# A 21,000-instruction fp32 block on one core: halves, quarters and casts moved between engines at the stage joints

## What is computed

```python
# first_block
h = x
h += chunked_band_attention(rmsnorm(h, norm_mix[0]))              # 16 heads
h += sq_relu_mlp(rmsnorm(h, norm_mlp[0]), w1[0], w2[0])            # relu(h@w1)**2 @ w2, width 4096
h += rglru_block(rmsnorm(h, norm_mix[1]))                          # conv, gates, scan, gelu branch, @ w_o
h += sq_relu_mlp(rmsnorm(h, norm_mlp[1]), w1[1], w2[1])
x = rmsnorm(h, norm_final)
# second_block
y = rwkv7_time_mix(rms_norm(x, norm_pre[0]), ...) ; h = x + rms_norm(y @ w_out, norm_post[0])
h += rms_norm(sigmoid(h @ ple_gate[0]) * (p[0] @ ple_w[0]), ple_norm[0])
k, v = shared_kv(h); y = diff_attention_mix(rms_norm(h, norm_pre[1]), k, v, ...)
h += rms_norm(y @ w_out, norm_post[1])
h += rms_norm(sigmoid(h @ ple_gate[1]) * (p[1] @ ple_w[1]), ple_norm[1])
```

## Time and profile before

| | |
|---|---|
| median of 3 executions | 1169.71 us (1169.52 to 1169.93) |
| the profiled execution | 1173.79 us, its span 1172.0 us |
| mean granted TensorE clock in it | 0.988 of full |
| PE busy | 1113.3 us (95%), 8956 instructions |
| DVE, ACT, POOL busy | 475.7 us (41%), 540.0 us (46%), 707.8 us (60%) |
| DMA | 169.44 MB, 145 GB/s in the mean |
| products of line 203 (fillers) | 500 of a 128 x 128 constant by the page, 59.4 us busy |

### The profile page before, as it was taken

The page is one execution under the profiler, slowest core; times in us unless marked ns, Lnnn a source line. Parts: engine busy times, 40 slices in busy tenths (PEclk is TensorE's granted clock), DMA queues, the critical chain, the costliest instruction groups (busy, mean ns, idle before and its releaser), DMA issues. The chain is left out here.

```text
span 1172.0 us, 20965 instructions
## 1 busy us (share of the span) xinstructions
PE 1113.3 (95%) x8956; PEld 925.5 (79%) x8956; DVE 475.7 (41%) x647; ACT 540.0 (46%) x851; POOL 707.8 (60%) x443
## 2 busy tenths in 40 slices
PE   9999999999999899999999999899998889999895
PEld 8788799998899789989984445899847677777864
DVE  1125274333246646521137175535641350233332
ACT  6437364444458755544421151212222564559452
POOL 5975459988947599998820035300034849667770
PEclk9999999999999999999999998999999989999998
DMA  8661455555546355555572443000036425433240
GB/s 319 225 233 55 144 159 184 189 188 189 189 129 212 110 162 183 191 186 193 183 233 72 127 158 110 21 4 4 4 127 236 150 95 183 140 100 120 81 159 36
DMA packets 45852, 169.44 MB, mean 145 GB/s; under 512 B 5088, under 2 KB 5344, under 8 KB 45440
## 3 DMA queue, kind: packets, MB, share of 16 engines
q1 hardware_dynamic: 43312, 159.06, 41.3%
q0 software_dynamic: 2448, 9.05, 2.4%
HBM read 167.03 MB, written 1.05 MB: 143 GB/s over the span
## 5 line engine op out<-in xcount | busy, mean ns | idle before, releaser
L709 POOL TENSOR_TENSOR ring_r<-ring,high_r 128x512 fp32r<-128x512 f32 (+1 forms) x368 | 636.6, 1763 | 238.9 <-ACT high_r L868 223.8
L868 ACT CAST high_r<-ring 128x1024 fp32r<-128x1024 f32 x248 | 256.2, 1049 | 215.6 <-DMA ring<-w 213.5
L435 PE MATMUL psum<-x_high,high_r 128*128 128x256 f32 x640 | 182.4, 285 | 2.2 <-DVE x_low L290 2.2
L435 PE MATMUL psum<-x_low,high_r 128*128 128x256 f32 x640 | 181.1, 283 | 0.0
L435 PE MATMUL psum<-x_high,ring_r 128*128 128x256 f32 x640 | 181.1, 283 | 0.0
L409 PE MATMUL psum<-high_r,x_high 128*128 128x512 f32 x320 | 127.3, 398 | 2.5 <-POOL ring_r L709 1.5
L612 DVE TENSOR_TENSOR arena<-arena 128x512 f32<-128x512 f32 x32 | 54.8, 1713 | 179.6 <-ACT arena L588 179.5
L435 PEld LDWEIGHTS psum<-x_high,high_r 128*128 128x128 f32 x640 | 122.7, 192 | 3.5 <-issue 1.8
L409 PE MATMUL psum<-high_r,x_low 128*128 128x512 f32 x320 | 124.8, 390 | 0.0
L409 PE MATMUL psum<-ring_r,x_high 128*128 128x512 f32 x320 | 124.6, 389 | 0.0
L435 PEld LDWEIGHTS psum<-x_low,high_r 128*128 128x128 f32 x640 | 122.7, 192 | 0.5
(11 more groups left out here) (317 smaller groups left out, 1717.2 us busy)
## 6 DMA issues: line engine op xcount, KB each, us to landing
ring<-w SPq DMA_DIRECT2D x292, 512.0 KB, 3.4
row<-rows POOLq DMA_DIRECT2D x14, 512.0 KB, 7.1
arena<-relt SPq DMA_DIRECT2D x2, 1536.0 KB, 10.6
h<-x SPq DMA_DIRECT2D x1, 1024.0 KB, 5.0
arena<-lora POOLq DMA_DIRECT2D x2, 512.0 KB, 6.8
out<-h SPq DMA_DIRECT2D x1, 1024.0 KB, 4.0
con<-consts SPq DMA_DIRECT2D x1, 529.0 KB, 4.5
arena<-pT POOLq DMA_DIRECT2D x2, 256.0 KB, 4.8
```

Source lines behind the costliest of these rows:

```text
L435: ins = nc.tensor.matmul(out, a, b, start=(k == 0 and q == 0), stop=(k == KT - 1 and q == 2))
L709: ins = nc.gpsimd.tensor_tensor(low(m)[:, part], raw(m)[:, part], read(high(m))[:, part], ALU.subtract)
L868: nc.scalar.copy(high(m), raw(m)).then_inc(high_made, 1)
```

## The change

1. **MLP ends.** The last four `w2` pieces are multiplied bank by bank: (tile 0, half 0), (0, 1), (1, 0), (1, 1), twelve products each, and each bank is announced by itself. The four pieces are released in the last of these. VectorE adds, ScalarE sums squares by half tile, VectorE finishes tile 0's statistics and scales it, and TensorE transposes tile 0 and then tile 1; fillers of 22 and 31 become 6 and 16. Behind the second MLP the two norms' roots are taken together, and transposes go to four banks instead of two.
2. **Recurrent block's end.** `a` squared and the casts of pieces `y6`, `y7` and the first of `W_RO` move from ScalarE to VectorE; ScalarE's tanh needs no settling wait. The first half's products with the gelu branch stand before the second half's scans; ScalarE's remaining casts lie between its gelus. GpSimd makes `W_RO`'s first low part without waiting for the scans. The filler of 34 and the wait before it are gone.
3. **Time mix.** The products of line 1939 come in three groups of 12, 12 and 8 instructions, each after a piece of `v`. `T_YA` is transposed, evacuated and used by halves, its first half ahead of the last gate piece; the filler of 8 is gone.
4. **Embedding.** The loop over the two rows of `p` is outside, that over the column halves inside, both column halves read from pieces 0 and 1; `piece_used` rises by 1 after the first row and by 3 after the second. Of pieces 2 and 3 eight columns are loaded.
5. **Rows.** GpSimd loads gain rows 11 to 13 later, in its list of the second attention.
6. **Second attention's end.** The first half of the heads is gated and transposed inside the loop, the SiLU of the last gates comes after the last heads' scaling, ScalarE's last two casts after the heads' root; GpSimd's `combine(7)` and `gate_rows(1)` move one piece forward; the filler of 30 becomes 5 and that of 16 is gone; the projection takes the halves as they come.
7. One filler of 7 in the chunk core becomes 8.

```diff
+UNUSED_PIECES = {4 * n + i for n in (W_PLE0, W_PLE1) for i in (2, 3)}
@@ mlp_act
-            split_until(min(w2_piece(m, 7, 3) + 1 + AHEAD, 4 * W_RKVG))
+            split_until(min(w2_piece(m, 7, 0) + RING, 4 * W_RKVG))
@@ mlp_pe
+            for t in range(NT):
+                for half in range(2):
+                    for f in range(4):
+                        piece_ready(pe, w2_piece(m, 7, f))
+                        pe.wait_ge(z_low, 16 * m + 14 + f // 2 + 1)
+                        ins = w2_product(m, 7, f, t, half)
+                        if (t, half) == (1, 1):
+                            ins.then_inc(piece_used, 1)
+                    if (t, half) != (1, 1):
+                        ins.then_inc(w2_part, 1)
@@ gpsimd
-            low_until(4 * W_RO)
+            low_until(4 * W_RO + 1)
...
-            for r in range(10, 14):
-                load_row(r)
+            load_row(10)
...
-                                   (33, combine, 6), (35, combine, 7), (36, gate_rows, 1)):
+                                   (33, combine, 6), (34, combine, 7), (35, gate_rows, 1)):
@@ scalar, recurrent block
-                settle(ins)
-                nc.scalar.activation(bb_[:, 4 * q:4 * q + 4, :], aa[:, 4 * q:4 * q + 4, :], ACT.Square).then_inc(g_ready, 1)
+                ins.then_inc(g_ready, 1)
...
+            made[0] = 4 * W_RO + 1
+            act.wait_ge(high_made, SPLITS[4 * W_RO + 1])
+            branch(0)
+            branch(1)
+            split_until(4 * W_RO + 3)
+            og_high_part(0)
+            og_high_part(1)
+            branch(2)
+            split_until(4 * W_RO + 5)
+            branch(3)
@@ vector, recurrent block
+                dve.wait_ge(a_ready, q + 1)
+                settle(nc.vector.tensor_tensor(bb_[:, u, :], aa[:, u, :], aa[:, u, :], ALU.mult))
...
+                for m in ((REC_AT["y6"], REC_AT["y7"]), (4 * W_RO,))[q]:
+                    cast_piece(m)
...
+                if q == 0:
+                    og_product(0)
+                    og_product(1)
@@ scalar, gates
-                split_until(4 * W_OUT_A + 4 * j + 4)
+                split_until(4 * W_OUT_A + 2 * j + 4)
+                evacuate_high(act, T_YA, (XH, None), blocks=(2 * j, 2 * j + 1))
@@ tensor
-            hold_clock(4, 22)
-            pe.wait_ge(xn_ready, 1)
-            pe_transposes(pe, T_N2, xn)
+            for t in range(NT):
+                if t == 1:
+                    hold_clock(0, 6)
+                pe.wait_ge(xn_ready, t + 1)
+                pe_transposes_of_tile(pe, T_N2, xn, t)
...
-            pe.wait_ge(gates_read, 4)
-            hold_clock(4, 34)
...
-                for c in range(2):
-                    for k in range(2):
-                        m = 4 * tile + 2 * c + k
-                        piece_ready(pe, m)
+                for k in range(2):
+                    m = 4 * tile + k
+                    piece_ready(pe, m)
+                    piece_ready(pe, m + 2)
+                    for c in range(2):
                         for t in range(NT):
                             ins = nc.tensor.matmul(psum[:, 2 * c + t, :], pT_sb[:, k, t * P:(t + 1) * P],
                                                    raw(m)[:, c * HALF:(c + 1) * HALF], start=(k == 0), stop=(k == 1))
-                        ins.then_inc(piece_used, 1)
+                    ins.then_inc(piece_used, 2 * k + 1)
...
-            hold_clock(0, 8)
-            pe_linear(pe, W_OUT_A, 2, xT2, None, transposed(pe, T_YA))
+            out_piece(W_OUT_A, T_YA, 0)
+            pe.wait_ge(y_ready, 2)
+            pe_transposes(pe, T_YA, yN, blocks=(2, 3))
+            for i in (1, 2, 3):
+                out_piece(W_OUT_A, T_YA, i)
+            pe_chunk(pe, W_OUT_A + 1, 1, xT2, None)
...
-                        hold_clock(4, 30)
+                        pe.wait_ge(od_ready, 1)
+                        pe_transposes(pe, T_OB, oD, blocks=(0, 1))
```

More of the change, by code:

```diff
@@ L203, in hold_clock, with pe_transposes @@
                 nc.tensor.matmul(psum[:, bank, 0:P], sq, sq, start=True, stop=True)
[L205 to L206 removed]
+        def pe_transposes(pe, inst, src, ready=None, blocks=range(4)):
+            for b in blocks:
                 if ready is not None:
@@ L217, in pe_transposes, with pe_transposes_of_tile @@
                 ins.then_inc(tp_filled, 1)
+        def pe_transposes_of_tile(pe, inst, src, t):
+            for b in range(4):
+                g = 4 * inst + b
+                if t == 0 and PREVIOUS[g] is not None:
+                    bank_out(pe, PREVIOUS[g])
+                for j in range(2):
+                    ins = nc.tensor.transpose(psum[:, BANK_OF[g], (2 * j + t) * P:(2 * j + t + 1) * P],
+                                              src[:, t, (2 * b + j) * P:(2 * b + j + 1) * P], ident)
+                if t == 1:
+                    ins.then_inc(tp_filled, 1)
         def pe_transpose_pair(pe, inst, i, src, b):
@@ L259, in evacuate, with evacuate_high @@
             ins.then_inc(tp_act if on_act else tp_dve, 1)
-        def evacuate_high(act, inst, *pairs, between=None):
-            for b in range(4):
+        def evacuate_high(act, inst, *pairs, between=None, blocks=range(4)):
+            for b in blocks:
                 g = 4 * inst + b
@@ L275, in evacuate_high, with evacuate_low @@
                     between(b)
-        def evacuate_low(dve, inst, *triples):
-            for b in range(4):
+        def evacuate_low(dve, inst, *triples, blocks=range(4)):
+            for b in blocks:
                 g = 4 * inst + b
@@ L623, in mlp_dve, with part_of, w2_product @@
             settle(nc.vector.tensor_tensor(root[:, 2 * i:2 * i + 2], r2, r2, ALU.mult))
-            for t in range(NT):
-                if t == 0:
-                    dve.wait_ge(w2_tile0, m + 1)
+            def part_of(t, c):
+                if (t, c) != (1, 1):
+                    dve.wait_ge(w2_part, 3 * m + 2 * t + c + 1)
                 else:
                     used_piece(dve, w2_piece(m, 7, 3))
-                for c in range(2):
-                    part = h[:, t, c * HALF:(c + 1) * HALF]
-                    ins = nc.vector.scalar_tensor_tensor(out=part, in0=psum[:, 2 * t + c, :],
-                                                         scalar=root[:, 2 * i + t:2 * i + t + 1], in1=part,
-                                                         op0=ALU.mult, op1=ALU.add)
-                ins.then_inc(h_tile0 if t == 0 else h_ready, 1)
+                part = h[:, t, c * HALF:(c + 1) * HALF]
+                nc.vector.scalar_tensor_tensor(out=part, in0=psum[:, 2 * t + c, :], scalar=root[:, 2 * i + t:2 * i + t + 1],
+                                               in1=part, op0=ALU.mult, op1=ALU.add
+                                               ).then_inc(h_ready if (t, c) == (1, 1) else h_tile0, 1)
+            return part_of
+        def w2_product(m, c, f, t, half):
+            n, hf = w2_piece(m, c, f), slice(half * HALF, (half + 1) * HALF)
+            pairs = parts([z[:, c % 2, f, t * P:(t + 1) * P] for z in (zh, zl)], (high(n)[:, hf], low(n)[:, hf]))
+            for q, (a, b) in enumerate(pairs):
+                ins = nc.tensor.matmul(psum[:, 2 * t + half, :], a, b, start=(c == 0 and f == 0 and q == 0),
+                                       stop=(c == 7 and f == 3 and q == 2))
+            return ins
         def mlp_pe(pe, m, inst):
@@ L1315, in row_of @@
                 return row[:, r % 5, :]
-            rms(2)
-            normed(xn, 2)
+            for t in range(NT):
+                for c in range(2):
+                    add_part(t, c)
+                dve.wait_ge(tail_sq, 2 * t + 2)
+                tail_sum(0, 2, t)
+                k = slice(4 + t, 5 + t)
+                nc.vector.tensor_scalar(var[:, k], ss[:, k], 1.0 / D, EPS, ALU.mult, ALU.add).then_inc(tail_var, 1)
+                dve.wait_ge(tail_root, t + 1)
+                settle(nc.vector.reciprocal(rstd[:, k], root[:, k]))
+                dve.wait_ge(*part_added(0, t, 1))
+                nc.vector.tensor_scalar(xn[:, t, :], h[:, t, :], rstd[:, k], None, ALU.mult).then_inc(xn_ready, 1)
             nc.vector.memset(xb[:, :, 0:3], 0.0).then_inc(pad_zero, 1)
@@ L2132, in _ @@
             state_outputs(1)
-            for n in range(2, 8):
+            for n in range(2, 7):
                 gate_piece(n // 4, n % 4)
+            pe.wait_ge(y_ready, 1)
+            pe_transposes(pe, T_YA, yN, blocks=(0, 1))
+            gate_piece(1, 3)
             def embed_pe(tile, e_n, T):
```

230 lines of the change are left out of this document (134 added, 96 removed).

## The result

The changed kernel takes **1157.39 us** (median of 4, 1155.4 to 1158.67) against 1169.82 beside it: ratio 0.989, interval 0.987 to 0.991. The forecast was 1148.5, range 1139.5 to 1157; the time lies 0.4 us above the range's end. The profiled execution took 1158.53, span 1156.7: the trace is 15.3 us shorter, the medians 12.4, because the trace of before was of an execution 4.1 us above its median and this one is 1.1 above.

What follows compares the result with a forecast made beforehand. TensorE's one dependent chain was taken as the bound, with gains only at joints and clock falls. Terms -28.4, +2.1 and +5.1 gave -21.2, so 1152.6 on the profiled scale, less 4.1: 1148.5 us, range 1139.5 to 1157.

Steps and rivals of the forecast that it cites:

- first MLP's end: Joint from first MLP to recurrent block: tile 0's statistics and scaling hidden under products, 8.6 to 5.8-5.9 us, -2.7.
- recurrent block's end: Joint behind the last input product: shorter ScalarE chain, earlier GpSimd run, third piece near 401 instead of 407.5, -6.7 us.
- second MLP's end, chain: Joint from second MLP to first mixture product: shorter statistics chain and new banks, 13.3 to 9.2 us, -4.1.
- clock there: One more clock fall counted for shorter fillers at MLP ends and before the last heads, +1.7 us.
- chunk ends: Line 1939's products, split in three, keep the clock up; gain limited by GpSimd before the transposes, -2.7 us.
- first output projection: First half transposed under the gates, first piece run while the second half is gated, 28.1 to 23.9 us, -4.2.
- second output projection: SiLU and two casts move behind the last heads; six pieces end at 1114.8 instead of 1122.7, -8.0 us.
- first embedding, with clock: First embedding: earlier start mostly given back by late refill, cast and copy, -0.6; clock fall, +1.7 us.
- second embedding, with clock: Second embedding: second piece freed late, so refill, cast and copy come later, +2.7; clock fall, +1.7 us.
- Rival 2: Clock falls at most joints, twice as long as counted: +8.5 us, time 1157; chance 0.15.
- Rival 1: Embeddings not late: ScalarE's copy waits for something else or the refill hides; time 1142.4 us; chance 0.20.
- Rival 3: GpSimd gives the recurrent block's gain back in the second MLP as its bound: +6.7, 1155 us; chance 0.08.

Runs made afterwards that it cites:

- scalar_work: Changed kernel with the recurrent block's end's two squares and three casts back on ScalarE, first half's products and casts still early; 1156.16 us, ratio 0.987.
- no_low_b: Changed kernel without GpSimd's low parts of the recurrent output projection's first two pieces, the high part used twice instead; 1151.05 us, ratio 0.982.
- after_again: The changed kernel itself measured and profiled once more, nothing changed; 1157.81 us, ratio 0.988 to the kernel before.
- ends_together: Changed kernel with the 32 two-column chunk-end products in one block again, behind the second v piece; 1158.47 us, ratio 0.989.
- two_first: Changed kernel, but at both embeddings ScalarE casts only two landed pieces before copying the products out, the others afterwards; 1144.27 us, ratio 0.976.
- fill_three: Changed kernel with fillers restored or lengthened at the recurrent block's end, second MLP's end and second output projection; 1158.97 us, ratio 0.988.
- copy_first: Changed kernel, but at both embeddings ScalarE copies the eight products out before casting further weight pieces; 1151.44 us, ratio 0.982.
- best_low: two_first plus longer second-MLP-end fillers, with VectorE making the low parts of the recurrent output projection's first two pieces; 1143.29 us, ratio 0.976.

## Why the prediction was right or wrong

On the scale of the trace the forecast was -21.2 and the measured difference is -15.3; one trace on each side. By its terms:

| term | forecast | measured | from |
|---|---|---|---|
| first MLP's end | -2.7 | -2.9 | 8.63 to 5.74 |
| recurrent block's end | -6.7 | -1.6 | 18.8 to 17.2 |
| second MLP's end, chain | -4.1 | -4.4 | 13.30 to 8.89 |
| clock there | +1.7 | +3.1 | window 611.00 |
| chunk ends | -2.7 | -2.7, and 2.8 behind it | 20.67 to 17.99 |
| first output projection | -4.2 | -4.6 | 28.2 to 27.0, less a gate piece of 3.4 that now runs inside |
| second output projection | -8.0 | -5.7 | 40.2 to 34.6 |
| first embedding, with clock | +1.1 | +2.2 | 18.0 to 19.9, gate at half clock |
| second embedding, with clock | +4.4 | +4.6 | 14.6 to 19.2 |

(The rest, -0.5: -0.4 ahead of the first MLP's end, -0.3 up to the second attention's last projections, +0.2 in the last gate products.)

- **First MLP, second MLP's chain, first output projection, second embedding**: right, in size and mechanism.
- **Recurrent block: the step that failed.** "VectorE takes squares and casts in its waits for ScalarE" and "hides up to about 2 us each behind the roots": it did take them in its waits, but beside GpSimd squares of 1.2 us last 2.3, and the waits were used up (scalar_work). The roots, forecast to end 5.9 us ahead of the last input product (388.73 - 382.8), end 3.5 ahead (385.39 - 381.87), 1.9 before the change. "GpSimd ... starts at about 396.7", 8.0 after that product, was the sum of engines that don't hold each other up; without its own two pieces beside VectorE it starts at 8.7 (no_low_b), with them at 12.7. (The term was also mis-added: 396.7 + 4.5 is 401.2, 6.3 and not 6.7 us before 407.50.) The Trainium skill, "SBUF — State Buffer", section "Who interferes with whom", says that a VectorE instruction with two SBUF inputs contends with a GpSimd instruction that reads SBUF; the trace agrees (2.44 against 4.47 us). The prediction weighed the page's other rule, on casts in a two-port mode, and asked only whether GpSimd would be held up, not VectorE. The row that it gave for that rule, 5.66 us beside the bias add, is of this kind: the bias add has two inputs and is no cast.
- **Second output projection**: the chain is as forecast (first piece 7.8 us behind the last projection piece, forecast 8.0; third 16.4, forecast 16.0). The 2.3 short are the clock, at 0.51 under the third and fourth piece (1.7), and 0.6 of later starts; kernels in which it stayed up took 33.0 instead of 34.6 us.
- **Clock**: direction right, size short. Three falls at 1.7 were counted; the windows show four, three of them 6.8 us long, worth up to 3.4 each. The recurrent block's own stretch (10.2 us) lies under a wait for GpSimd in this trace, in that of after_again partly not. Rival 2 was of this kind, but that its 1157 is the measured time is luck: the clock is some 4 us of the miss, not 8.5.
- **Chunk ends**: right to the transposes, with the short wait named. The further 2.8 us up to the gates are no edit's gain that could be shown: from these transposes to the gates it is 126.3 us before and 123.6 after, but 125.9 in the changed kernel's second trace, 125.0 in ends_together, and between 123.5 and 126.5 in all the variants. Why it varies is left open. That the stretch was short in this trace is luck; without it the miss would be larger.
- **First embedding**: the late copy was right, but the cast ends 0.5 us later than forecast, the hole is 5.05 us instead of about 4.4, and the clock under the filler and the first gate products makes up the rest.
- **Rival 1** fell: the embedding is late. Times near its 1142.4 came only where the lateness was taken away (two_first, 1144.3). **Rival 3** didn't occur: TensorE's time in the second MLP is the same to 0.1 us.
- **The median**: of the 8.9 us between 1148.5 and 1157.39, 5.9 are the terms above and 3.0 the scale: the difference was reckoned from a profiled execution 4.1 us above its median, and the one after is only 1.1 above its own.

## What to carry to other kernels

Work moved to an idle VectorE isn't free where GpSimd runs: put one GpSimd instruction's wait beside each two-input instruction of VectorE, and see whether the "idle" time survives. Ask of each in-order queue what stands ahead of the one instruction that others wait for: here a cast that waited for a refill cost 13 us and one changed line gave it back. A filler ahead of a first hole can make the next one longer, as in fill_three (1.40 to 3.98 us), and the clock then falls behind that one; a filler in the last hole of that joint was not tried.

## What was not expected of the hardware

- Both engines are slowed, and the single instructions say how: they take turns. VectorE's low part at 392.61 ends 0.55 us after GpSimd's half that ran from 392.04 to 393.82, so it takes 1.76 instead of 0.69 us; GpSimd's next half, from 393.78, ends 1.14 us after that low part and takes 1.73 instead of 1.27. So it goes in every pair of the stretch, with scans (0.66 to 1.7) and with a cast (0.68 to 1.79). By the sums: four scans 2.44 to 4.47 us, scaled adds 2.74 to 6.28 for four (copy_first), GpSimd's two halves 2.53 to 3.5 to 3.9. One GpSimd piece of two halves thus costs VectorE about 2.1 us, more than the 1.22 in which VectorE makes it itself (best_low).
- The clock behind the same short holes was 0.53 in one execution and 1.00 in another of the same kernel. The Trainium skill, "TensorE: Matmul & The Clock Gate", Part 1, says that the chip's activity window runs free of the kernel; that agrees with the two traces here, though no run here could set its phase.
